# Who copies the weight chunks into the window, and in what order: all twelve on VectorE

## The reference, cut to what matters

```
logits = h @ w_router + b_router ; top 4 ; gates = softmax of the four
for each block of rows that one expert e has to do:
    gu  = xb @ w_gate_up[e] + b_gate_up[e]          # 1024 -> 2048
    gt  = min(gu[:, :1024], 7) ; up = clip(gu[:, 1024:], -7, 7)
    act = (up + 1) * (gt * sigmoid(1.702 * gt))
    out = (act @ w_down[e] + b_down[e]) * gate      # 1024 -> 1024
    y[tokens] += out
x = x + gt_f * y ; result = rmsnorm(x, g_final)
```

## Time and profile before

| | us |
|---|---|
| Median of three runs (1581.17 to 1583.4) | 1581.21 |
| The profiled execution: its time | 1582.56 |
| its span in the trace | 1580.7 |
| PE busy in the span | 1371.7 |
| DVE busy | 901.2 |
| ACT busy | 652.0 |
| VectorE's 366 copies into the window | 438.8 |
| ScalarE's 180 copies into the window | 338.3 |

### The profile page before, as it was taken

The page is one execution under the profiler, slowest core; times in us unless marked ns, Lnnn a source line. Parts: engine busy times, 40 slices in busy tenths (PEclk is TensorE's granted clock), DMA queues, the critical chain, the costliest instruction groups (busy, mean ns, idle before and its releaser), DMA issues.

```text
span 1580.7 us, 23063 instructions
## 1 busy us (share of the span) xinstructions
PE 1371.7 (87%) x6259; PEld 552.8 (35%) x6259; DVE 901.2 (57%) x1452; ACT 652.0 (41%) x720; POOL 236.3 (15%) x156
## 2 busy tenths in 40 slices
PE   4798998499999978999799879999999889869971
PEld 2586467333333322333233223333333223223320
DVE  3999696855455544564464445655555455446546
ACT  3434551144445433443444335444444344344432
POOL 1740252111010100101001101101111100100111
PEclk9899989699999988999899899999999999989986
DMA  9757023659898999399989981899899989998993
GB/s 378 238 191 254 25 107 125 221 203 379 307 383 315 376 390 364 113 383 381 389 307 385 390 302 20 312 352 336 327 367 384 382 303 378 382 389 308 386 350 120
DMA packets 207172, 474.36 MB, mean 300 GB/s; under 512 B 18482, under 2 KB 18994, under 8 KB 206130
## 3 DMA queue, kind: packets, MB, share of 16 engines
q1 hardware_dynamic: 196322, 455.24, 77.5%
q0 software_dynamic: 10832, 18.90, 5.3%
HBM read 463.07 MB, written 18.35 MB: 305 GB/s over the span
## 4 chain that ended last, share of the span: by engine, by line
SPq 38%; PE 22%; DMA 16%; DVE 11%; issue 9%; ACT 2%; DVEq 0%; POOL 0%; ACTq 0%; POOLq 0%
SPq L314 29%; DMA ring<-in_w_down 11%; PE ps L1449 10%; SPq L317 7%; PE ps L1461 4%; DVE bc L845 4%; DMA wm<-in_w_mod 2%; DMA xg<-h_rows,idx_n 2%; DVE window L998 1%; DMA ring<-in_w_gate_up 1%; PE ps L1327 1%; PE ps L1351 1%; PE ps L1353 1%; PE ps L1352 1%; PE ps L1441 1%
## 5 line engine op out<-in xcount | busy, mean ns | idle before, releaser
L1449 PE MATMUL ps<-window,xT 128*64 128x512 f32 x2880 | 663.6, 614 | 6.3 <-DVE window L998 6.3
L998 DVE COPY window<-ring 128x2048 f32<-128x2048 f32 x366 | 438.8, 1223 | 180.7 <-DMA ring<-in_w_gate_up 116.9
L733 ACT ACTIVATE window<-ring 128x2048 f32<-128x2048 f32 x180 | 338.3, 1905 | 232.9 <-DMA ring<-in_w_gate_up 125.1
L1461 PE MATMUL ps<-window,aT 128*64 128x512 f32 x1440 | 351.0, 620 | 0.0
L1449 PEld LDWEIGHTS ps<-window,xT 128*64 128x64 f32 x2880 | 204.0, 141 | 396.9 <-issue 379.5
L1135 DVE TENSOR_SCALAR gb<-ps 128x256 f32<-128x256 f32 x90 | 38.1, 423 | 218.3 <-PE ps L1449 216.3
L540 POOL DMA_INDIRECT y_rows<-osb,idx_c x46 | 80.8, 1756 | 546.3 <-ACT osb L723 533.4
L1461 PEld LDWEIGHTS ps<-window,aT 128*64 128x64 f32 x1440 | 93.5, 140 | 156.7 <-issue 153.0
L527 POOL DMA_INDIRECT xg<-h_rows,idx_n x46 | 46.2, 1004 | 595.3 <-DVE idx_n L1028 595.3
L1471 PE MATMUL ps<-csb,ab 128*128 128x128 f32 x180 | 42.2, 319 | 90.4 <-DVE ab L1142 90.2
L720 ACT ACTIVATE aT<-ps 128x256 f32<-128x256 f32 x90 | 34.5, 384 | 191.0 <-PE ps L1471 191.0
(11 more groups left out here) (278 smaller groups left out, 1219.1 us busy)
## 6 DMA issues: line engine op xcount, KB each, us to landing
ring<-in_w_gate_up SPq DMA_DIRECT2D x512, 512.0 KB
ring<-in_w_down SPq DMA_DIRECT2D x128, 1024.0 KB, 13.5
wm<-in_w_mod SPq DMA_DIRECT2D x4, 2048.0 KB, 21.6
wm_a<-in_w_mod SPq DMA_DIRECT2D x4, 2048.0 KB, 9.1
wm_b<-in_w_mod SPq DMA_DIRECT2D x4, 2048.0 KB, 8.6
win<-in_w_in SPq DMA_DIRECT2D x3, 2048.0 KB, 20.1
x_in<-in_x SPq DMA_DIRECT2D x1, 2048.0 KB, 10.5
wo_f<-in_w_out SPq DMA_DIRECT2D x1, 2048.0 KB, 7.6
```

What stands on the lines that cost most here:

```text
L733: A(window[c % NW][:, :, :, :], ring[:, c, :, :, :], ACT.Copy).then_inc(S["moved_by_act"], 1)
L998: V.tensor_copy(window[c % NW][:, :, :, :], ring[:, c, :, :, :]).then_inc(S["moved_by_dve"], 1)
L1449: last = MMUL(ps[M * j:M * (j + 1), h, :].rearrange("m (g n) -> m g n", g=2), xT[:, k, :], window[c % NW][:, k % CK, :, j * GW:(j + 1) * G ...
L1461: last = MMUL(ps[M * y:M * (y + 1), 2, :], aT[:, h, i, M * j:M * (j + 1)], window[c % NW][:, k % CK, y, :], start=False, stop=(h == 1 and ...
```

## The change

The two lists of line 322 and the two counters of finished copies go; one counter `moved` takes their place. ScalarE's `move` goes, with the value it read for it. VectorE copies all twelve chunks: 6, 7 and 8 after the small operations and ahead of `swiglu(1)`; 9, 10 and 11 after `swiglu(1)`; then `pick_expert`, and 0 to 5 of the next item. PE takes `act_to_channels(1)` between chunk 8 and chunk 9 instead of in the middle of chunk 9.

```diff
         def wait_moved(eng, c, item):
-            if c in BY_DVE:
-                eng.wait_ge(S["moved_by_dve"], len(BY_DVE) * item + BY_DVE.index(c) + 1)
-            else:
-                eng.wait_ge(S["moved_by_act"], len(BY_ACT) * item + BY_ACT.index(c) + 1)
+            eng.wait_ge(S["moved"], NCH * item + c + 1)
...
-            sp.wait_ge(S["moved_by_dve"], len(BY_DVE) * n + NW)
+            sp.wait_ge(S["moved"], NCH * n + NW)
...
                     A(table_kept[:, :], ones[:, 0:1], ACT.Sigmoid)
-                    move(6, p, b)
-                    move(7, p, b)
                     sigmoid(0, b)
                     copy_aT(0, b)
-                    move(10, p, b)
-                    move(11, p, b)
                     sigmoid(1, b)
...
                     swiglu(0, b)
-                    second(8)
-                    second(9)
                     dve.wait_ge(S["scattered"], 16 * b + 32)
...
                     numbers(b + 2)
+                    second(6)
+                    second(7)
+                    second(8)
                     swiglu(1, b)
-                    first_of_next(0)
-                    first_of_next(1)
+                    for c in range(9, NCH):
+                        second(c)
                     dve.wait_ge(S["bias_used"], b + 1)
                     pick_expert(b + 1)
-                    for c in range(2, NW):
+                    for c in range(NW):
                         first_of_next(c)
...
                     pe.wait_ge(S["aT_ready"], 2 * b + 1)
-                    down(0, 0, 3, b)
+                    down(0, 0, 2, b)
                     act_to_channels(1, b)
-                    down(0, 3, 4, b)
+                    down(0, 2, 4, b)
```

More of the change, by code:

```diff
@@ L300, in build @@
             lg_copied lg_turned m8_ready ex_ready mask_ready pos_done o_zero table_ready y_zero bias_ready
-            gate_free xg_zero dve_u slot_used moved_by_dve moved_by_act meta_done at_done xt_done
+            gate_free xg_zero dve_u slot_used moved meta_done at_done xt_done
             bias_used g_ready act_ready sel_ready idx_ready cur_ready pick_ready s_sig aT_ready
@@ L320, in landed_at @@
             return 32 if c < 8 else 16
-        BY_DVE, BY_ACT = (0, 1, 2, 3, 4, 5, 8, 9), (6, 7, 10, 11)
         def wait_moved(eng, c, item):
-            if c in BY_DVE:
-                eng.wait_ge(S["moved_by_dve"], len(BY_DVE) * item + BY_DVE.index(c) + 1)
-            else:
-                eng.wait_ge(S["moved_by_act"], len(BY_ACT) * item + BY_ACT.index(c) + 1)
+            eng.wait_ge(S["moved"], NCH * item + c + 1)
         def pair(i):
@@ L727, in sigmoid @@
                 A(sg[:, :], gb[:, :], ACT.Sigmoid, scale=ALPHA).then_inc(S["s_sig"], 1)
[L729 to L733, removed]
             copy_xT(1)
@@ L743, in _ @@
                 with act.If(b < n):
-                    p = act.value_load(item_p[0:1, bass.ds(b, 1)], min_val=0, max_val=NE - 1)
                     A(table_kept[:, :], ones[:, 0:1], ACT.Sigmoid)
-                    move(6, p, b)
-                    move(7, p, b)
                     sigmoid(0, b)
                     copy_aT(0, b)
-                    move(10, p, b)
-                    move(11, p, b)
                     sigmoid(1, b)
@@ L997, in move @@
                 dve.wait_ge(w_ld[c], landed_at(c) * p + landed_at(c))
-                V.tensor_copy(window[c % NW][:, :, :, :], ring[:, c, :, :, :]).then_inc(S["moved_by_dve"], 1)
+                V.tensor_copy(window[c % NW][:, :, :, :], ring[:, c, :, :, :]).then_inc(S["moved"], 1)
             residual(0)
```

## The result

| | us | runs |
|---|---|---|
| changed kernel, median | 1589.62 (1582.46 to 1592.71) | 9 |
| kernel before, beside it | 1581.85 (1581.17 to 1585.84) | 9 |
| ratio | 1.0037, 95% interval 1.0020 to 1.0054 | |

The forecast was 1570.0 with a range of 1563 to 1586. The changed kernel's runs spread over 10 us, the other's over 5, so a few us of one profiled execution (1589.62, span 1587.8) are not to be read by themselves; repeated patterns are.

What follows compares the result with a forecast made beforehand. Bound: a chain of DMA stretches and SP's waits for VectorE's copy of chunk 0. Terms +3.7 - 9.1 - 1.65 - 1.15 - 4.2 + 1 = -11.4 us gave a 1570 us median, 8 in 10 within 1563 to 1586.

Steps and rivals of the forecast that it cites:

- the chain: SP's expert loads: DMA stretch to the last landing, then a wait for the copy of chunk 0, ten times, and tail.
- the step from the copy of 11 to the restart: After two-item experts, VectorE's copy of 11, pick_expert, copy of 0, SP's issue: 2.93 us, against 4.23 before.
- The first load: First load inside the loop, behind item 0's copy of chunk 0: 3.67 us later, bounds 3.4 and 4.2.
- A DMA stretch has the length of its bytes: Loads between pauses: 34 to 35 us per expert, not altered by the change.
- the 9.1 us: Gain at the seven restarts after experts of two items, 1.30 us each.
- `swiglu(1)` is done before the last landing, since it needs chunk 7 only, which lands four chunks earlier: Before restarts after two-item experts: only VectorE's copy of 11, pick_expert and copy of 0 remain after the last landing.
- My last rival: The wait isn't shortened: swiglu(1) still late, with chunk 8's copy ahead of it; ruled out, given no chance.
- the 3.07 us from the last copy to PE's end: From the start of the copy of 11 until PE finishes the item: 3.07 us, against 8.40 before.
- the terms for three items, four items and the tail: Gains of 1.65 us and 1.15 us at the restarts after those experts, and 4.2 us in the tail.
- so the other side does get its turn: POOL's scatter beside VectorE's back-to-back copies of chunks 3 to 5: delayed only 0.6 us, bounds 0.5 and 1.8.
- locked out: Rival, chance 0.24: POOL waits for the last copy; four cycles of two loads take 77.6 us; about 1581 us.
- the margin of 0.1 us at chunk 6: Scatter lands 9.4 us into an item, VectorE comes to it at 9.5, so PE hardly waits for chunk 6.

Runs made afterwards that it cites:

- e4: Kernel before, with ScalarE's sigmoid of the second half ahead of its copy of chunk 11: 1566.07 us, ratio 0.9880.
- e2: Changed kernel, with VectorE's copy of the next item's chunk 0 right behind 9, ahead of 10 and 11: 1566.04 us, ratio 0.9878.
- e3: Kernel before, with PE's part of the change alone (act_to_channels(1) between chunks 8 and 9): 1590.99 us, ratio 1.0043.
- e6: Changed kernel, with PE's old order put back (act_to_channels(1) in the middle of chunk 9): 1589.32 us, ratio 1.0039.
- e1: Changed kernel, with VectorE's copies of chunks 6 and 7 ahead of its wait for the scatter: 1587.01 us, ratio 1.0011.
- e7: Changed kernel, with pick_tokens behind the copies 6 to 8 instead of ahead of swiglu(0): 1585.06 us, ratio 1.0008.
- e10: Changed kernel, with copies 6 and 7 ahead of the scatter wait and pick_tokens moved behind swiglu(0) and the copies 6 to 8: 1585.72 us, ratio 1.0000.
- e8: Kernel before, VectorE also copying chunk 10 behind the next chunk 0, ScalarE copying 6, 7, and 11 behind its second-half sigmoid and aT: 1569.50 us, ratio 0.9909.

## Why the prediction was wrong, step by step

**Right: the chain.** DMA stretch, wait for the copy of chunk 0, DMA stretch. e4 and e2 moved that copy and nothing else of weight, and won 19 us over the kernel before and 25 over the changed one. In the changed kernel's cycles of two loads the way through the scatter's landing is about as long.

**Right: the step from the copy of 11 to the restart.** In the three pauses in which that copy waited for its landing it was 2.90, 2.91 and 2.91 us (such as 806.30 to 809.21), with 2.93 forecast. The first load came 4.22 later, with 3.67 forecast, just at the bound of 4.2.

**Wrong, and half of the miss: "A DMA stretch has the length of its bytes", "The change moves no byte".** I put the change of this term at 0, though I had named a changed length as what would show my reading to be wrong. In the same three pauses of the changed kernel the copy of 11 began 73.73, 141.54 and 140.97 us after the restart before it, where it was 71.50, 139.71 and 140.18 in the kernel before (486.63, 797.58 and 1285.11, ScalarE's). The trace's DMA records have the last packet of the loads for every stretch:

| us | before | after |
|---|---|---|
| seven cycles: restart to the last packet, sum | 704.1 | 711.4 |
| seven cycles: last packet to the next restart, sum | 34.0 | 26.2 |
| the two long cycles: restart to the last packet | 139.5, 139.5 | 141.0, 141.0 |

So the seven pauses gave 7.8 of the 9.1 us, and the stretches took 7.2 back; with the long cycles the stretches make 10.2 of the 20.0 us of the miss. It is no chance of one profile. With chunks 6, 7, 10 and 11 on ScalarE the first sum is 704.1, 706.9 (e3) and 704.1 (e4); with all chunks on VectorE and chunk 0 behind 11 it is 711.4, 712.7 (e6), 712.6 (e1), 713.4 (e7) and 713.3 (e10).

Why they are longer stays open in part. Loads that start later behind a late copy of chunk 6 account for little of it: 132 us after the restarts at 657.87 and 664.76 the loads had moved 47.76 and 47.61 MB, and after those at 1144.93 and 1153.96 47.95 and 47.97. The time goes in the last microseconds of a stretch. Here are both kernels at its end, the kernel before first, from 137.0 us after the restart on:

```profile
794.87:795.87 1.00, 1.00 (x4) 0.24 (x2) 0.00 (x0) 0.89 (x1) 0.73 (x1) 0.50 0.81 324
795.87:796.87 1.00, 1.00 (x7) 0.16 (x3) 0.00 (x0) 1.00 (x1) 0.26 (x1) 0.98 0.66 201
796.87:797.87 1.00, 1.00 (x7) 0.47 (x7) 0.85 (x3) 0.31 (x2) 0.00 (x0) 1.00 0.52 156
...
801.76:802.76 1.00, 1.00 (x5) 0.38 (x5) 0.65 (x2) 0.19 (x1) 0.00 (x0) 1.00 1.01 266
802.76:803.76 1.00, 1.00 (x6) 0.29 (x4) 0.93 (x4) 0.23 (x1) 0.00 (x0) 1.00 0.87 283
803.76:804.76 1.00, 0.97 (x6) 0.20 (x2) 1.00 (x2) 0.00 (x0) 0.00 (x0) 1.00 0.53 217
804.76:805.76 1.00, 0.78 (x4) 0.34 (x6) 1.00 (x2) 0.38 (x1) 0.00 (x0) 1.00 0.17 70
```

And POOL's gather of the next rows, the kernel before first:

```profile
795.14 0.98 POOL L527 DMA_INDIRECT xg<-h_rows,idx_n  x1 [19.29 <-DVE idx_n L1028]
...
796.32 1.63 POOL L522 DMA_INDIRECT xg<-h_rows,idx_n  x1 [15.50 <-DVE idx_n L1012]
```

The change put the copies 6 to 8 behind `numbers`, where 8 and 9 had been ahead of it. So the gather is issued 131.6 us after the restart instead of 137.3, among the last loads instead of at their end, and lands after 7.5 us instead of 3.8. That fits the slower end, but no run moves the gather alone. It can't be the whole either: e8's sum is 711.2, with `numbers` still behind 9, though SP restarts sooner after the last packet there, so the two sums compare only roughly.

**Wrong: "`swiglu(1)` is done before the last landing, since it needs chunk 7 only, which lands four chunks earlier".** I took the landing of chunk 7 for its use. Between the two stand, in VectorE's order, the landing of 5 and its copy, 1.6 us of the loop's turn, `pick_tokens`, `swiglu(0)`, the small operations and three copies, and then PE at the lower clock. Measured in the item of the shown rows, 13.7 us go by from the start of copy 5 to the use of chunk 7. In the kernel before that was hidden: `swiglu(1)` waited for ScalarE's copy of 11 anyway. My last rival named it, and I ruled it out with "so this can't be". I gave the term no row, although the rows of before held it: PE's 5 us stalls for the first half's `ab` in DMA-bound items, and 16 matmuls in 5.8 us behind them. In the seven cycles it cost little: the last packet to the restart is 26.2 us in sum, and 24.5 in e10, where `swiglu(1)` is late at none. It weighs in the three other places, by the 3.07 us from the last copy to PE's end. In the item shown PE ended at 639.13 + 3.65 = 642.8, some 5 us after the copy of 11 starts at 637.7, as chunk 10 as well as 11 was still to do; in e10 it was 3.7. With that went the terms for three items, four items and the tail.

**Wrong: "so the other side does get its turn".** The row was of an instruction of POOL against additions of VectorE. Against copies in a row without a gap the scatter waits for the last and ends 1.44 to 1.47 us after it. This was my rival "locked out"; the margin of 0.1 us at chunk 6 was gone, and e1, which takes the wait for the scatter away from chunk 6, wins about 4 us. Its cycles of two loads were to be 77.6; they are 75.1 to 76.6. The Trainium skill, "SBUF — State Buffer", "Who interferes with whom", has the rule as an exclusive lock for a whole instruction. The trace of the changed kernel agrees with it, and adds that POOL gets no turn between two copies either. I had set it behind a row that showed something else.

**Not weighed: PE's own part of the change.** I put it in as a cover for chunk 9 at 0.43 us an item. e3 shows that it costs 0.43% of the time on the kernel before. In the changed kernel taking it back wins nothing (e6); that it is one of several waits there, of which only the longest counts, is argued.

## What to carry to other kernels

When a stage waits for a landing, don't date a step by when its data lands, but follow each engine's queue to it, with the loop's turn and the clock after a stall: in a queue worked in order, the step is as late as the latest landing ahead of it. When work is moved to one engine to free another, ask which instruction restarts the bounding resource, and put that one first: here two lines of order were worth 19 us and moving 180 copies nothing. And a margin of 0.1 us is not cover. Last, a stretch that the DMA engines bound keeps its bytes but not its length: compare it between the two traces before looking for the loss elsewhere. Here a gain of 8 us at the pauses was there, and longer stretches hid it.

## What the runs showed of the hardware

- A POOL indirect DMA that starts under VectorE copies without a gap ends 1.44 to 1.47 us after the last of them (2.86 and 4.62 us instead of 1.57). If a gap or a late first copy let its generation begin, it ends 0.08 to 0.09 us after the copy that came in between (such as the one at 1057.39, 2.34 us). A VectorE operation with two SBUF inputs has the first effect too (6.06 us).
- The same weight loads took 139.0 to 139.7 us per four experts in the kernel before and 140.3 to 141.0 in the changed one.
- A stall of PE costs twice: after 2.13 and 1.51 us of standing still 16 matmuls took 6.38 us at a granted clock of 0.50, against 3.65 at 1.00; after a stall of 1.14 they took 3.65.
- The form of a copy matters: 128x2048 float32 takes 1.22 us as a copy on VectorE, 1.91 as an activation, and 2.28 as a maximum with itself.
